# Separate sum buffers for down, a gate convolution that accumulates in PSUM, and low parts of g cut earlier

## The reference

```
gu = rms_norm(x, g) @ w_in            # 1024 -> 2 * 2816
a, up = jnp.split(gu, 2, axis=-1)
full = jnp.concatenate([prefix, a], axis=1)
c = conv_b + sum(conv_w[r] * full[:, r:r + t] for r in range(CONV_W))   # CONV_W = 3
y = (jax.nn.silu(c) * up) @ w_down    # 2816 -> 1024
x = x + y
```

## Time and profile before

| | us |
|---|---|
| three runs | 2359.24, 2364.98, 2372.10 |
| median | 2364.98 |
| profiled execution: time, span in the trace | 2369.25, 2367.5 |
| TensorE busy | 2143.7 (91% of the span) |
| VectorE busy | 1570.4 (66%) |
| GpSimd busy | 1399.2 (59%) |
| ScalarE busy | 844.8 (36%) |

### The profile page before, as it was taken

One profiled execution on the slowest core, in us unless ns is written; L12 is line 12 of the kernel. 1 busy time (PEld: TensorE's weight loads), 2 busy tenths in 40 slices (PEclk: granted clock), 3 DMA queues, 4 the chain that ended last, 5 costly groups with the idle time before them and its releaser, 6 DMA issues.

```text
span 2367.5 us, 41687 instructions
## 1 busy us (share of the span) xinstructions
PE 2143.7 (91%) x16730; PEld 2025.2 (86%) x16730; DVE 1570.4 (66%) x2160; ACT 844.8 (36%) x1640; POOL 1399.2 (59%) x1227
## 2 busy tenths in 40 slices
PE   9999999889999997778899999989999999778889
PEld 8986699889989896777879988989899899777777
DVE  7356765978877875454665356498788788654455
ACT  6317943333233332232252236253333233322220
POOL 1005636778878875665642223578788788556663
PEclk9999999999999997999999999999999999889999
DMA  5313001222232134333111130112222322523312
GB/s 189 108 66 132 2 31 35 73 82 86 80 107 87 71 125 146 100 101 107 48 45 53 45 116 22 45 37 93 94 86 80 107 85 70 178 83 112 106 64 95
DMA packets 80322, 200.68 MB, mean 85 GB/s; under 512 B 7788, under 2 KB 36452, under 8 KB 76776
## 3 DMA queue, kind: packets, MB, share of 16 engines
q1 hardware_dynamic: 77304, 189.16, 23.4%
q10 hardware_dynamic: 2832, 8.94, 1.0%
HBM read 153.63 MB, written 46.48 MB: 85 GB/s over the span
## 4 chain that ended last, share of the span: by engine, by line
PE 35%; POOL 33%; issue 11%; DMA 8%; ACT 8%; DVE 4%; SPq 0%; POOLq 0%; ACTq 0%; DVEq 0%
POOL w_lo L784 16%; POOL w_sum L799 15%; DMA raw<-in_w 7%; PE ps L1483 5%; PE ps L1004 5%; PE ps L1006 5%; PE ps L1005 5%; PE ps L1485 5%; PE ps L1484 5%; PE ps L1571 2%; ACT w_hi L1641 2%; POOL ssq L773 2%; ACT g_hi L1641 1%; DVE g_lo L2613 1%; ACT s_exp L1860 1%
## 5 line engine op out<-in xcount | busy, mean ns | idle before, releaser
L1641 ACT ACTIVATE w_hi<-w_sum 128x512 fp32r<-128x512 f32 (+1 forms) x336 | 176.6, 526 | 1037.1 <-POOL w_sum L799 979.5
L1483 PE MATMUL ps<-t_hi,w_hi 128*128 128x264 f32 x1408 | 413.9, 294 | 62.7 <-POOL w_lo L784 49.1
L784 POOL TENSOR_TENSOR w_lo<-w_sum,w_hi 128x512 fp32r<-128x512 f32 (+1 forms) x336 | 411.4, 1229 | 77.9 <-ACT w_hi L1641 67.9
L1483 PE MATMUL ps<-g_hi,w_hi 128*128 128x264 f32 x1120 | 338.3, 302 | 125.7 <-DVE x L2812 83.1
L1485 PE MATMUL ps<-t_hi,w_lo 128*128 128x264 f32 x1408 | 405.4, 288 | 0.0
L1484 PE MATMUL ps<-t_lo,w_hi 128*128 128x264 f32 x1408 | 405.3, 288 | 0.0
L784 POOL TENSOR_TENSOR w_lo<-raw,w_hi 128x512 fp32r<-128x512 f32 (+1 forms) x252 | 333.3, 1336 | 26.0 <-ACT w_hi L1641 25.8
L1483 PEld LDWEIGHTS ps<-g_hi,w_hi 128*128 128x128 f32 x1120 | 226.1, 202 | 135.3 <-DVE x L2812 89.8
L1483 PEld LDWEIGHTS ps<-t_hi,w_hi 128*128 128x128 f32 x1408 | 270.6, 192 | 77.9 <-POOL w_lo L784 37.3
L1004 PE MATMUL ps<-h_hi,w_hi 128*128 128x352 f32 x1008 | 331.2, 329 | 6.5 <-DVE h_lo L2222 6.0
L1484 PE MATMUL ps<-g_lo,w_hi 128*128 128x264 f32 x1120 | 332.6, 297 | 0.0
(11 more groups left out here) (269 smaller groups left out, 4858.0 us busy)
## 6 DMA issues: line engine op xcount, KB each, us to landing
raw<-in_w SPq DMA_DIRECT2D x141, 512.0 KB, 4.0
g_f<-g_spill SPq DMA_DIRECT2D x70, 528.0 KB, 5.8
g_spill<-c_buf SPq DMA_DIRECT2D x20, 1056.0 KB, 4.0
raw<-in_w SPq DMA_DIRECT2D x82, 256.0 KB, 3.0
g_spill<-t_buf SPq DMA_DIRECT2D x20, 792.0 KB, 6.5
s_mk<-in_s_mk SPq DMA_DIRECT2D x2, 2048.0 KB, 9.5
s_mv<-in_s_mv SPq DMA_DIRECT2D x2, 2048.0 KB, 14.0
out_y<-x ACTq DMA_DIRECT2D x7, 528.0 KB
```

What stands on the lines that cost most here:

```text
L784: pool.tensor_tensor(block_of(flat_lo, j), whole, block_of(flat_hi, j).bitcast(F32), ALU.subtract) \
L1483: pe.matmul(out, hi_w[:, k, :], hi_x[:, k, t0:t0 + HC], start=begin, stop=False, skip_group_check=True)
L1641: return act.activation(out, in_, ACT.Copy)
```

## The change

1. The sums of down's weights leave the ring `w_sum` from the second pair of down on. Odd pairs write them into `s1`, even pairs into `t_buf` (`sum_of`). These two buffers are the ones that gate and up use, so the first use of each waits until that work is done: for `s1` all products of up taken, for `t_buf` all three multiplications by up. The wait for product j - 8 is left out for these sums; it stays for the high and low parts.
2. The prompt part of the gate convolution is written by ScalarE into PSUM banks 6 and 7 (`c_prompt`), both taps of VectorE add to it there, and SiLU reads it from there. SiLU is now two instructions (1024 and 32 columns). As there is one such buffer for both blocks, `tap2` of block 1 waits for SiLU of block 0, and the first product of down waits for the last SiLU. In ScalarE's order `tap2` of block 1 and both SiLUs move later; in VectorE's the third-tap instruction of block 0 moves ahead of the first addition of the up pair, and `scale` of block 1 behind the last.
3. In the last up pair of a layer VectorE cuts the first four low parts of g between its other work, and the last three multiplications by up move from the first pair of down to places that reach into the second (`LAST_UP`).
4. The last three additions of squares on GpSimd ahead of the feed-forward part move behind `pair_middle` of its first pair, and the copy of that pair's first product goes to `c_buf` instead of `s1`, whose place the squares still hold.

```diff
+LAST_UP = [(0, 5), (1, 0), (1, 2)]
...
+        def sum_of(j, name):
+            pair = j // NPROD
+            if pair <= NPAIR:
+                return block_of(flat_sum, j)
+            at = DB * ["S1", "S2", "S4", "S3"].index(name)
+            flat = sums_odd if (pair - NPAIR) % 2 == 1 else sums_even
+            return flat[:, at:at + DB].rearrange("p (m n) -> p m n", m=GPAIRS)
...
+        c_prompt = banks(6, 2, SEQ)
+        def first_of(n):
+            return c_buf[:, 1, 0:HT] if n == 0 else s1[:, n % 2, :]
...
             def sum_block(l, pair, j, name, a, b, op, after=None):
-                slot_free(l, j)
+                if pair <= NPAIR:
+                    slot_free(l, j)
+                if pair == NPAIR + 1:
+                    pool.wait_ge(taken, 6 * NPAIR * (l + 1))
+                if pair == NPAIR + 2:
+                    pool.wait_ge(up_scaled, 3 * NG * (l + 1))
                 if after is not None:
                     pool.wait_ge(w_summed, sums(l, pair, after))
-                pool.tensor_tensor(block_of(flat_sum, j), a, b, op).then_inc(w_summed, 1)
+                pool.tensor_tensor(sum_of(j, name), a, b, op).then_inc(w_summed, 1)
...
                     if oo == KD - 1:
                         pair_first(l, 0)
-                    if oo >= 1:
+                    if 1 <= oo < KD - 1:
                         add_squares(w, range(NCH * (oo - 1), NCH * oo))
             def low_ffn(l, w):
                 pair_middle(l, 0)
+                add_squares(w, range(NCH * (KD - 2), NCH * (KD - 1)))
                 pair_last(l, 0)
...
+                        if pos == 0 and p == 0:
+                            pe.wait_ge(silued, NF * (l + 1))
...
-                act.activation(c_buf[:, s, TS:T], a_buf[:, s, TS:T], ACT.Identity, bias=cc[:, 3:4], scale=cc[:, 2:3])
+                if s == 1:
+                    act.wait_ge(silued, NF * l + f)
+                act.activation(c_prompt, a_buf[:, s, TS:T], ACT.Identity, bias=cc[:, 3:4], scale=cc[:, 2:3])
...
-                act.activation(c_buf[:, s], c_buf[:, s], ACT.Silu).then_inc(silued, 1)
+                act.activation(c_buf[:, s, TS:T], c_prompt, ACT.Silu)
+                act.activation(c_buf[:, s, 0:TS], c_buf[:, s, 0:TS], ACT.Silu).then_inc(silued, 1)
...
-                    c_p = c_buf[:, s, TS + back:T]
+                    c_p = c_prompt[:, back:SEQ]
```

More of the change, by code:

```diff
@@ L2769, in up_pair @@
                     tap(i, 0, 1)
+                    tap(i, 0, 2)
                     product_done(n, 1)
@@ L2782, in up_pair @@
                     plus(2, t_buf[:, 1, :])
+                    if i == NG - 1:
+                        low_g(l, 0, 0)
                     scale(i, 0)
@@ L2787, in up_pair @@
                     TT(halves_of(out[:, 0, first]), chain_banks(0), halves_of(c_buf[:, 0, first]), ALU.mult).then_inc(taken, 1)
-                    scale(i, 1)
+                    if i == NG - 1:
+                        low_g(l, 0, 1)
                     product_done(n, 6)
                     p1_plus(n, 2, t_buf[:, 2, :])
+                    scale(i, 1)
+                    if i == NG - 1:
+                        low_g(l, 0, 2)
+                        low_g(l, 0, 3)
                     dve.wait_ge(c_scaled, NF * l + 2 * i + 2)
@@ L2818, in down_pair @@
                             low_g(l, 0, 4 + pos)
-                        if p == 0 and pos >= 3 and pos < 6:
-                            e = (3, 4, 6)[pos - 3]
-                            times_up(NPAIR - 1, NG - 1, (0, 1, 1)[pos - 3], (second, second, first)[pos - 3], pos - 3, e)
+                        if (p, pos) in LAST_UP:
+                            t = LAST_UP.index((p, pos))
+                            times_up(NPAIR - 1, NG - 1, (0, 1, 1)[t], (second, second, first)[t], t, (3, 4, 6)[t])
                         if g + 1 < NGRP and (q, pos) in G_AT:
@@ L2836, in ffn @@
                     up_pair(i)
-                for k in range(4):
-                    low_g(l, 0, k)
                 for p in range(DPAIRS):
```

24 lines of the change are left out of this document (13 added, 11 removed).

## The result

| kernel | runs | median, us | lowest to highest |
|---|---|---|---|
| before | 4 | 2363.01 | 2359.24 to 2372.10 |
| after | 4 | 2239.60 | 2236.70 to 2243.06 |

The ratio is 0.9473, with a 95% interval from 0.9442 to 0.9504. The profiled execution of the changed kernel took 2236.70 us (span 2235.0) against 2369.25 (2367.5). The forecast was 2231.

A forecast was written before the change was run, and what follows sets the result against it. It took down to lose most per microsecond, through a slot of the sum ring and a lowered clock. 49 + 13 + 6 + 1 = 69 us per layer, 138 in all, from 2369.25 gave 2231 us, range 2195 to 2280.

The forecast's parts named there:

- The pairs after the start: Down, products 13 to 114: separate sum buffers remove the waits behind GpSimd's ring slot, saving 49 us per layer (20 to 53).
- The margin of 0.2 us: Down's later pairs: VectorE's addition is done at T+8.6, product 6 wants it at T+8.8.
- T: Start of a pair p in down, six products ahead of the point where TensorE stopped; the chain's instants count from it.
- The start of down: Down up to product 13: earlier sums and low parts save 13 us per layer (5 to 14.5); one 6 us stall stays.
- The convolution in PSUM: Gate and up: taps of 1.25 us instead of 1.73, 0.6 us less per round, 6 us per layer over 10 rounds.
- Squares: Ahead of gate and up: TensorE's 4.17 us wait for the first low sum goes; 1 us saved per layer (-2 to 4).
- The shrunken chain: Rival, down: waits only shrink, 3 us per group plus a fallen clock of 1.5 us remain; 2270 us, chance 0.18.
- More in gate and up: Rival: GpSimd, not VectorE, closes the loop there, so its 2 to 3.5 us per round come through; 2195 us, chance 0.12.
- Sums that don't decide: Rival, down: weights are the limit, DMA waits replace slot waits, only the start gains 10 us a layer; 2350 us, chance 0.06.
- Slower: Rival: same-bank PSUM reading and writing in gate and up costs 145 us and loses the 12 won; 2388 us, chance 0.04.
- A half rate in PSUM: Gate and up: an instruction reading and writing the same bank runs at half rate, 1.1 us more for each of 88 taps.
- The foretold 215 us for 20 pairs: Down: a sign that the forecast is right, 20 pairs taking about 215 us.

The follow-up runs named there:

- e1_sums_only: Kernel before, with only the sums of down's weights from the second pair on moved out of the ring into s1 and t_buf; 2235.89 us.
- e2_old_ring: Changed kernel, with only the sums of down's weights put back into the ring; 2363.14 us, ratio 0.9984 to before.
- e3_g_first: Kernel before, with ScalarE in down making due high parts of g ahead of the weights' high part, ring unchanged; 2296.99 us.
- e4_one_buffer: Changed kernel, with the sums of all pairs of down from the second on in s1, t_buf not used for them; 2226.76 us.

## Why the prediction came out right

The total was 9 us off. Part of this is luck in the starting point: the 138 us foretold were taken from the profiled execution of 2369.25, which lies 6 us above the median of 2363.01. The two profiled executions differ by 132.6 us, the two medians by 123.4. By its own steps:

*The pairs after the start, 49 us per layer.* Measured 48.8 in layer 0 and 51.0 in layer 1. The margin of 0.2 us held: behind product 13 no wait is longer than 0.5 us in layer 0. The steps came as they were worked out. At the first of the places that stalled (product 41, which waited 5.65 us before), with T at 971.89, ScalarE's g is done at T+6.7 (foretold T+6.7), VectorE's low part at T+8.0 (T+7.9), and the product starts at 980.68, T+8.8 (T+8.8), without a wait; at the same place in the next two groups the wait is 0.13 and 0.16 us:

```profile
977.48 1.07 ACT L1667 ACTIVATE g_hi<-g_f 128x1056 fp32r<-128x1056 f32 x1
...
978.58 1.26 DVE L2643 TENSOR_TENSOR g_lo<-g_f,g_hi 128x1056 fp32r<-128x1056 f32 x1 [1.39 <-ACT g_hi L1667]
979.75 1.93 DVE L2849 TENSOR_TENSOR x<-x,ps 128x528 f32<-128x528 f32 x3
```

e1_sums_only and e2_old_ring show that this is the ring, and e3_g_first that half of what it costs goes by moving g ahead on ScalarE.

*The start of down, 13 us.* Measured 11.4 in layer 0 and 8.5 in layer 1, the term that was most overestimated. Product 6 came at 921.09 (922 foretold), product 13 at 937.47 (938.5), its wait 5.88 (about 6), GpSimd's start on the third pair at 928.69 (929.6). That these instants agree is in part luck: they were worked out with the end of up at 903.49, and it came 4.1 us earlier. Counted from the end of up, product 13 starts at 38.1 us, where 35.0 were foretold and 49.5 was the old value. Two details were wrong. SiLU ended at 906.14, not at 909, and product 0 gained 0.2 us against the end of up, not 1.5, because one wait took the other's place. And I gave the early low parts of g a share that isn't theirs: with part 1 alone the start shrinks by 15.1 us, with parts 2 and 3 alone by 2.4, with all three by 11.4. Beside part 1, parts 2 and 3 cost 3.7 us there, since they put off the last multiplications by up, for which GpSimd now waits. e4_one_buffer takes this back.

*The convolution in PSUM, 6 us per layer.* The traces of before and after differ by 14.4 us over both layers, 7 per layer, but that pair proves little: the four kernels with the old convolution have the same code there and lie between 937.9 and 946.8. The mean of the four is 941.6, that of the four with PSUM 933.6. So I put the edit at 8.0 us in all, where 12 were forecast, with a scatter about as large. What stood behind the number fits the traces: the tap took 1.27 us, GpSimd's gain became slack (its waits for `raw` rose from 117.8 to 150.2 us in the whole run), and the loop through SyncE's store was the other end. With that loop opened, the two convolutions are 9.4 to 12.1 us apart, and kernels with the same one within 2.1. The worth is that of PSUM and the new order together; in SBUF the new order makes these rounds 55.8 us longer (993.7 against 937.9).

*Squares, 1 us.* This came out with the other sign. Of the 4.17 us of the earlier trace rows 0.50 is left, but 1.86 us for the low part of T2 and 3.31 for `ssq` stand in its place. From the first matmul of gate (395.32 before, 395.26 after) to the first wait for `a_buf` are 35.07 us before and 36.54 after; the old code has 35.1 in six traces, the new one 35.6 to 36.5. So it costs 0.5 to 1.5 us, inside the bounds.

```profile
403.87 0.39 PE L1507 MATMUL ps<-t_hi,w_hi 128*128 128x264 f32 x1 [1.86 <-DVE t_lo L2623]
410.37 2.68 PE L1070 MATMUL ps<-ssq,ones 128*128 128x352 f32 x4 [3.31 <-POOL ssq L791]
```

This is also why e1_sums_only equals the whole change. In down part 1 alone gives 64.9 us in layer 0, the whole change 60.2. What parts 2 and 3 win in the rounds (11.2 us between these two traces) goes for the later start of down (4.7 us in a layer) and the head (0.5 to 1.5). The total of the forecast was near; its share for parts 2 and 3, 12 us and a part of the 13 per layer, was not there in the sum.

*The rivals.* The shrunken chain is out (no repeated waits). More in gate and up is out as a forecast of this change, but what it named, a round near the 41.2 us of TensorE, came as 41.90 with another order on SyncE. Sums that don't decide is out by e1_sums_only. Slower is out by the time itself. A half rate in PSUM is out by the tap's 1.27 us. The foretold 215 us for 20 pairs was a slip: from 906.24 to 1128.47 are 222.2, and my own terms gave 220.

## What to carry to other kernels

Follow a wait back to the first engine that had nothing to do, and look at what stands ahead of each step on every engine it passes: there were two ways to cut into this chain. The sums in other buffers gave 132 us, and one order changed on ScalarE gave 71 us without a buffer. Order on a queue is worth a look before buffers and places are: a store and a load that changed places gave 51 us, four times what the faster convolution was forecast to give in the stage that they closed. Before crediting a few microseconds to an edit in one trace, see how far traces of the same code differ there.
